# Second FFN of a two-block transformer: last gate product of a phase kept in its product banks, and one-instruction low parts for the plain down-projection's weights

## The reference, cut to what matters

```python
h = rmsnorm(x, norm_ffn_pre[l])
f = (jax.nn.silu(h @ ffn_w_gate[l]) * (h @ ffn_w_up[l])) @ ffn_w_down[l]
x = x + rmsnorm(f, norm_ffn_post[l])
```

## Time and profile before

| | |
|---|---|
| median of 3 runs | 1759.29 us (1759.22 to 1760.31) |
| the profiled execution, its own time | 1759.92 us |
| its span, first to last instruction | 1758.1 us |
| outside the span | 1.8 us |
| mean granted TensorE clock | 0.998 |
| PE busy | 1735.3 us of the span |
| POOL, DVE, ACT busy | 1165.9, 897.3, 597.4 us |

### The profile page before, as it was taken

The page is one execution under the profiler, slowest core; times in us unless marked ns, Lnnn a source line. Parts: engine busy times, 40 slices in busy tenths (PEclk is TensorE's granted clock), DMA queues, the critical chain, the costliest instruction groups (busy, mean ns, idle before and its releaser), DMA issues.

```text
span 1758.1 us, 25603 instructions
## 1 busy us (share of the span) xinstructions
PE 1735.3 (99%) x9543; PEld 1451.0 (83%) x9543; DVE 897.3 (51%) x1583; ACT 597.4 (34%) x1196; POOL 1165.9 (66%) x1241
## 2 busy tenths in 40 slices
PE   7999999999999999999999999999999999999998
PEld 5786768899899887878888888777888888998997
DVE  6447666764165254262005373555433569773753
ACT  3236663355065122222014232554300222450542
POOL 6643558957657786666766665554778599677574
PEclk9999999999999999999999999999999999999999
DMA  6620012323323232223332222212233222324231
GB/s 220 211 75 28 25 49 101 105 96 109 108 82 110 98 114 90 83 72 100 100 100 71 75 73 86 66 68 73 73 99 106 84 90 88 111 86 132 75 115 64
DMA packets 48075, 163.10 MB, mean 93 GB/s; under 512 B 5614, under 2 KB 8750, under 8 KB 47696
## 3 DMA queue, kind: packets, MB, share of 16 engines
q1 hardware_dynamic: 46744, 158.28, 27.1%
q10 hardware_dynamic: 1208, 3.18, 0.6%
HBM read 158.41 MB, written 2.11 MB: 91 GB/s over the span
## 4 chain that ended last, share of the span: by engine, by line
PE 93%; DVE 2%; POOL 1%; ACT 1%; issue 1%; DMA 1%; ACTq 0%; SPq 0%; DVEq 0%; POOLq 0%
PE bank L980 92%; POOL w_lo_t L3066 1%; PE bank L1384 1%; PE bank L1430 1%; DMA x_sb<-in_x 0%; POOL w_hi_t L3061 0%; DMA kv_raw<-att_l_t 0%; DVE sq_sum L2176 0%; ACT h_hi L1879 0%; ACT sq L1645 0%; DVE x_sb L2625 0%; DVE sig L2305 0%; DVE cmp_xt L2615 0%; ACT att_pt L2022 0%; DVE h_lo L2424 0%
## 5 line engine op out<-in xcount | busy, mean ns | idle before, releaser
L3066 POOL TENSOR_TENSOR w_lo_t<-w_raw,w_hi_t 128x256 fp32r<-128x256 f32 (+1 forms) x809 | 690.1, 883 | 18.1
L3061 POOL TENSOR_SCALAR w_hi_t<-w_raw 128x1024 fp32r<-128x1024 f32 (+1 forms) x217 | 243.9, 1124 | 386.3 <-PE bank L980 351.6
L980 PE MATMUL bank<-h_hi,w_hi_t 128*128 128x512 f32 (+1 forms) x1192 | 434.9, 365 | 9.1 <-ACT h_hi L1879 8.3
L980 PE MATMUL bank<-h_hi,w_lo_t 128*128 128x512 f32 (+1 forms) x1192 | 423.7, 356 | 0.0
L980 PE MATMUL bank<-h_lo,w_hi_t 128*128 128x512 f32 (+1 forms) x1192 | 420.1, 355 | 0.4 <-DVE h_lo L2424 0.3
L980 PEld LDWEIGHTS bank<-h_hi,w_hi_t 128*128 128x128 f32 x1192 | 226.3, 190 | 51.6 <-issue 19.2
L980 PEld LDWEIGHTS bank<-h_lo,w_hi_t 128*128 128x128 f32 x1192 | 225.4, 189 | 34.1 <-issue 1.7
L980 PEld LDWEIGHTS bank<-h_hi,w_lo_t 128*128 128x128 f32 x1192 | 226.4, 190 | 31.1 <-issue 1.2
L980 PE MATMUL bank<-hid_hi,w_hi_t 128*128 128x512 f32 (+1 forms) x439 | 170.4, 388 | 1.7 <-DVE hid_lo L2309 0.9
L980 PE MATMUL bank<-hid_lo,w_hi_t 128*128 128x512 f32 (+1 forms) x439 | 169.6, 386 | 0.0
L980 PE MATMUL bank<-hid_hi,w_lo_t 128*128 128x512 f32 (+1 forms) x439 | 169.6, 386 | 0.0
(11 more groups left out here) (424 smaller groups left out, 3121.8 us busy)
## 6 DMA issues: line engine op xcount, KB each, us to landing
w_raw<-in_w SPq DMA_DIRECT2D x261, 512.0 KB, 3.4
w_more<-in_w SPq DMA_DIRECT2D x15, 512.0 KB, 3.6
y<-in_w SPq DMA_DIRECT2D x6, 512.0 KB, 5.3
x_sb<-in_x SPq DMA_DIRECT2D x4, 512.0 KB, 7.4
x_sb<-in_x ACTq DMA_DIRECT2D x1, 1536.0 KB, 6.7
u_raw<-in_w SPq DMA_DIRECT2D x2, 512.0 KB, 5.4
toep<-table SPq DMA_DIRECT2D x4, 256.0 KB
decay<-in_decay SPq DMA_DIRECT2D x1, 1024.0 KB, 4.8
```

The source lines that it names most:

```text
L980: return pe.matmul(out, lhs, rhs, start=start, stop=stop, **kw)
L3061: pool.tensor_scalar(hi[:, 0:cols], src[:, 0:cols], 1.0, 0.0, ALU.mult, ALU.add).then_inc(*did("w_hi", i))
L3066: ins = pool.tensor_tensor(lo[:, piece], src[:, piece], hi.bitcast(F32)[:, piece], ALU.subtract)
```

## The change

Two parts.

1. `IN_PIECES` ends ahead of the slots of `("down2", 0)`: the low part of each of these seven slots is one L3066 of 1024 columns instead of four of 256.
2. The last gate product of a paired phase (once in phase 1, once in phase 2) is made in the banks "c" and "d". The sigmoid of the right half is written into bank "c" by ACT; DVE multiplies it there by the product of up and gate; the up product's left half is added up in bank "d" and multiplied there by the gate. The high and low parts are then made for each half of 256 columns by itself (ACT from the bank, DVE from the bank and the high part), and the low part releases the bank. PE's wait ahead of the last block is for the release of bank "d". The product L2300 in SBUF stays.

```diff
-IN_PIECES = range(SLOTS["cqr"][0], SLOTS[("pair2", 1, 0)][0])
+IN_PIECES = range(SLOTS["cqr"][0], SLOTS[("down2", 0)][0])
...
+    def pair_half(name, b):
+        return ps((name, b))[:, 0:T // 2]
+
     def gate_low(name):
-        return after("hid_d2" if name[2] == PARTS2[name[1]] - 1 else "hid_p2", name)
+        return evacuated((name, "d")) if name[2] == PARTS2[name[1]] - 1 else after("hid_p2", name)
...
+        def last_gate(name):
+            act.wait_ge(*after("prod_d2", name, "gate"))
+            act.activation(pair_half(name, "c"), gate_rows(name)[0][:, RIGHT], ACT.Sigmoid).then_inc(*did("sg", name, 1))
+            for b, side in (("c", RIGHT), ("d", LEFT)):
+                act.wait_ge(*after("prod_d2", name, b))
+                act.activation(hid2[0][:, name[2], side], pair_half(name, b), ACT.Copy).then_inc(*did("hid_s2", name, b))
...
                 gate_left(last)
-                gate_right(last)
-                act.wait_ge(*after("prod_d2", last, 0))
-                act.wait_ge(*after("prod_d2", last, 1))
-                gate_high(last, gate_rows(last)[2])
+                last_gate(last)
...
             dve.wait_ge(*after("st_pe", name, Q_S4))
-            dve.tensor_tensor(to, u2_t, pair_bank(name, "c"), ALU.add).then_inc(*release((name, "c")))
+            dve.tensor_tensor(to, u2_t, pair_bank(name, "c"), ALU.add)\
+               .then_inc(*did("prod_d2", name, "gate") if last else release((name, "c")))
...
             g, s, u = gate_rows(last)
-            dve.wait_ge(*evacuated((last, "c")))
+            own("prod_d2", last, "gate")
             chain(dve.tensor_tensor(u[:, RIGHT], u[:, RIGHT], g[:, RIGHT], ALU.mult))
             own("sg", last, 1)
-            dve.tensor_tensor(u[:, RIGHT], u[:, RIGHT], s[:, RIGHT], ALU.mult).then_inc(*did("prod_d2", last, 0))
-            pair_c21(last)
+            dve.tensor_tensor(pair_bank(last, "c"), u[:, RIGHT], pair_bank(last, "c"), ALU.mult).then_inc(*did("prod_d2", last, "c"))
+            own("st_pe", last, Q_W22)
+            chain(dve.tensor_tensor(pair_bank(last, "d"), u2_t, pair_bank(last, "d"), ALU.add))
             dve.wait_ge(*evacuated((last, "a")))
-            dve.tensor_tensor(u[:, LEFT], u[:, LEFT], g[:, LEFT], ALU.mult).then_inc(*did("prod_d2", last, 1))
-            own("prod_d2", last, 0)
-            own("prod_d2", last, 1)
-            own("hid_s2", last)
-            dve.tensor_tensor(hid2[1][:, last[2]], u, hid2[0][:, last[2]].bitcast(F32), ALU.subtract)\
-               .then_inc(*did("hid_d2", last))
+            dve.tensor_tensor(pair_bank(last, "d"), g[:, LEFT], pair_bank(last, "d"), ALU.mult).then_inc(*did("prod_d2", last, "d"))
+            for b, side in (("c", RIGHT), ("d", LEFT)):
+                own("prod_d2", last, b)
+                own("hid_s2", last, b)
+                hi, lo = [h[:, last[2], side] for h in hid2]
+                dve.tensor_tensor(lo, pair_bank(last, b), hi.bitcast(F32), ALU.subtract).then_inc(*release((last, b)))
```

More of the change, by code:

```diff
@@ L448 @@
 o_ready o_hi m_ready gla_v gla_s gla_kd gla_st gla_a gla_done gla_t prod gate_s merged merged_hl q_s swa_neg swa_m swa_n swa_s swa_p swa_done ft lo_t table last_t last_x last_sum last_f last_r last_c last_l last_y first_hi first_lo
-st_h st_t st_xhi st_xlo st_s st_hi st_lo st_pe st_u2 st_q st_c22 hid_p hid_d st_r wq_hi sg prod2 prod_d2 g_right hid_s2 hid_p2 hid_d2""".split()
+st_h st_t st_xhi st_xlo st_s st_hi st_lo st_pe st_u2 st_q st_c22 hid_p hid_d st_r wq_hi sg prod2 prod_d2 g_right hid_s2 hid_p2""".split()
 class Counts:
@@ L1773, in gate_right, with gate_high @@
             act.activation(s[:, RIGHT], g[:, RIGHT], ACT.Sigmoid).then_inc(*did("sg", name, 1))
-        def gate_high(name, product):
-            act.activation(hid2[0][:, name[2]], product, ACT.Copy).then_inc(*did("hid_s2", name))
+        def gate_high(name):
+            act.wait_ge(*after("prod2", name))
+            act.activation(hid2[0][:, name[2]], gate_rows(name)[0], ACT.Copy).then_inc(*did("hid_s2", name))
+        def last_gate(name):
[4 more added lines that the diff above has]
+                act.activation(hid2[0][:, name[2], side], pair_half(name, b), ACT.Copy).then_inc(*did("hid_s2", name, b))
         def pair_phase(pairs):
@@ L1805, in pair_phase @@
                 else:
-                    act.wait_ge(*after("prod2", old))
-                    gate_high(old, gate_rows(old)[0])
+                    gate_high(old)
             last = pairs[-1]
@@ L2250, in pair_c22, with pair_c12 @@
             dve.tensor_tensor(to, q_t, pair_bank(name, "d"), ALU.add).then_inc(*did("st_c22", name))
-        def pair_c12(name):
+        def pair_c12(name, last=False):
             if name[0] == "pair":
@@ L2291, in pair_phase @@
             pair_c22(last)
-            pair_c12(last)
+            pair_c12(last, not up)
             if up:
```

## The result

The changed kernel takes 1766.96 us (median of 5 runs, 1766.09 to 1767.65) against 1759.22 for the kernel before beside it (5 runs, 1758.97 to 1760.31): a ratio of 1.0043, 95% interval 1.0028 to 1.0058. It is slower by 7.7 us, where 4.6 had been forecast, and 0.2 above the upper end of the range. The profiled execution took 1766.71, with a span of 1764.9. The changed source is a few lines longer: L980 of before is now L983, L3066 is L3075, L3061 is L3070, L2160 is L2167, L2551 is L2560, L2558 and L2559 are L2567 and L2568, L2562 is L2571, L2159 is L2166, L2319 and L2324 are L2328 and L2333, L2335 is L2344, L2300 is L2308, L2602 is L2611. L2319 of the changed source is the new low part of the gate product, which L2309 made before.

What follows compares the result with a forecast made beforehand. PE, busy 99%, bounds the kernel, with three small waits to win. 1759.92 + 4.9 (late copy) + 1.1 (clock) - 1.4 (gate product) = 1764.5 us, 1763.9 for the median; range 1759.0 to 1766.8.

Steps and rivals of the forecast that it cites:

- (a) to (e): Profile signs: long low parts, late chunk low part, 4.7 us wait for output 2's copy, no phase-end waits, half clock.
- Rival 1: The cover holds: DVE catches up before output 6 takes its bank, both parts win, 1756.9 us; chance 0.13.
- rival 2: Half the delay: one POOL turn fewer inside DVE's stretch, no fall of the clock, 1760.5 us; chance 0.12.
- rival 3: The full delay at output 6, but the clock stays at 1.00: 1762.8 us; chance 0.2.
- rival 4: The gate product gains nothing, from L2300 or the new chain meeting the lock: 1.4 more, 1765.3 us; chance 0.05.
- Step (b): Inputs of the paired phases: POOL's longer turns among eleven 1024-column DVE instructions add 3.0 us.
- step (a): Last hidden chunk of phase 0: DVE's last low part 2.4 us later, at 1475.4; PE waits 1.2 us.
- The walk: Following each DVE and POOL instruction under the lock from the last hidden chunk to output 6: +4.9 us.
- The clock: A likely fall to half clock after about 4.6 us of PE idle ahead of output 6: +1.1 us, bounds 0 and 1.7.
- rival 5: More is late: one more long part inside, or half clock beyond one stretch, 1766 to 1767.5 us; chance 0.1.

Runs made afterwards that it cites:

- p2_only: The changed kernel with the old IN_PIECES range, so only the gate product in the banks: 1757.76 us, ratio 0.9993.
- long_2: p2_only with the low part of slot 2 of ("down2", 0) in one instruction of 1024 columns: 1758.64 us, ratio 0.9995.
- long_0to1: p2_only with the low parts of slots 0 and 1 of ("down2", 0) in one instruction each: 1761.07 us, ratio 1.0008.
- p2_banks: p2_only with outputs 6 and 7 given the next two free banks, all seven low parts in pieces: 1757.41 us, ratio 0.9990.
- all_512: p2_only with all seven low parts of ("down2", 0) in two instructions of 512 columns: 1764.24 us, ratio 1.0026.
- long_3to6: p2_only with the low parts of slots 3 to 6 of ("down2", 0) in one instruction each: 1763.78 us, ratio 1.0026.
- p1_only: The kernel before with the new IN_PIECES range, so one-instruction low parts without the new gate product: 1767.59 us, ratio 1.0047.
- long_0to2: p2_only with the low parts of slots 0 to 2 of ("down2", 0) in one instruction each: 1761.43 us, ratio 1.0013.
- after_banks: The changed kernel with outputs 6 and 7 given the next two free banks, the four behind set aside: 1762.21 us, ratio 1.0018.

## Why the prediction was right and wrong

**Right.** The direction, the two places, the engine and the mechanism. (a) to (e) of its list came: low parts of 3.25 and DVE instructions of 3.4; the chunk's low part (L2160, now L2167) behind PE's need; a wait for the copy of output 2 in place of POOL's; no wait at the phase ends, with the low part 2.1 us ahead (1.7 forecast); a stretch at clock 0.50 behind 1505. The second part is worth its -1.4 by p2_only's median, though the interval just takes in no change, and by its trace, in which the waits at both phase ends are gone. Rival 1 (the cover holds) and rival 2 (half the delay) are refuted by the 6.4 us below, rival 3 (the clock stays at 1.00) by the two stretches at 0.50 in this execution, and rival 4 (the gate product gains nothing) by p2_only. Step (b) was put at +3.0 and measured 22.00 - 18.65 = +3.35.

**Wrong: the size of step (a).** The walk had the last chunk's low part end at 1475.4. It ended at 1477.28; the times of this execution lie 0.5 us later than before's from ahead of the changed code on (POOL's last low part ahead of these slots starts at 1455.79 for 1455.32), so 1476.8, a delay of 3.8 for 2.4, and PE's wait came to 2.6 for 1.2. What was missing is the pause between L2551 and L2558, in which ACT takes the sigmoid: 0.77 us idle in the row of L2567. The prediction doesn't print its walk, but followed again over these rows the chain ends at 1475.4 without that pause and at 1476.8 with it. With it, L2567 comes behind slot 2's high part, and L2568, with three instructions still to come, behind its low part; without it only the end of the chain meets that low part. The 1.4 us make 4.9 + 1.4 = 6.3 for output 6; the trace has 1506.74 - 0.5 - 1499.86 = 6.4. long_2 and long_0to1 tried the walk with the pause on new kernels: 0.3 and 1.6 us of wait for 0.5 and 1.8 expected.

**The clock** was put at +1.1. It fell twice in this stretch. The first fall, from 1478.87, slowed PE in a stretch that ended in the wait for the copy, and shortened that wait (3.0, where 4.7 had been forecast). The second, over PE's 1506.74 to 1509.59, cost half of 2.85, +1.4. The prediction had one fall, behind the copy. So much of rival 5 (more is late) came true.

**The sum** by the trace: 1758.1 + 0.5 + 6.4 + 1.4 - 1.4 = 1765.0, against a span of 1764.9. Of the 3.1 us by which the forecast was short, 1.5 stand at output 6 (6.4 for 4.9), 1.4 of them step (a); 0.3 are the clock, 0.5 the offset, and 0.85 that the changed kernel's median lies 0.25 above its profiled execution, where 0.6 below had been taken from before. The offset stands ahead of the changed code, and executions differ by as much the other way: in p2_banks, PE resumes behind POOL's wait at 1497.81, 0.56 earlier than before's 1498.37.

## What to carry to other kernels

Where two engines exclude each other for the length of an instruction, the price of merging one's instructions is paid by the other, and it reaches the critical engine wherever the other's chain has little cover; here 3 us of POOL's own work by the prediction's estimate, of which 1.0 counted, cost two waits of 2.6 and 3.2. When such alternation is followed, every hand-over inside the chain (here 0.77 us on ACT) has to be in it, because it decides which turn is missed. And when one late slot is the problem, change that slot alone, by as little as makes it timely.

## What the runs showed of the hardware

The lock works on instructions, not on time: DVE's two-operand instructions of 1024 columns waited 2.2 us (3.41 for 1.22) for a whole low part, and those of 512 columns 2.1 (2.77 for 0.69). This is what the Trainium skill says in "SBUF — State Buffer", section "SBUF: two separate sides", and the trace agrees. In all_512 halving POOL's instruction did nothing for a DVE that works without a pause (22.07 us for 22.00): from 1481.26 on, each of its instructions took 1.95 to 2.32 for 1.22, so POOL took a turn at each of them while it had work.

The clock did not follow the wait alone. In the changed kernel it fell to 0.50 (1.2 GHz) 1.5 us behind 2.6 us in which PE was idle, and again inside the 3.2 us of idle ahead of output 6, each time for 3.4 us. It fell inside an idle time of 4.7 us in all_512 and of 4.6 in long_3to6, for 6.83 us each. Behind the 2.6 us at the chunk it fell in every trace that has them (also p1_only, long_0to2 and after_banks). But p1_only, idle for 3.6 us ahead of output 6, went on at 1.00. The two windows there, the wait and what follows it:

```profile
1503.54:1507.35 3.81, 0.39 (x3) 0.01 (x1) 3.71 (x6) 0.00 (x0) 0.00 (x0) 1.00 0.79 323
1507.35:1510.80 3.45, 3.45 (x15) 2.83 (x16) 3.32 (x6) 0.00 (x0) 0.00 (x0) 1.00 0.00 0
```

What made the difference stays open; here a wait of 2.6 to 4.7 us cost 0 to 2.7 us more than itself.
